# Laying the weights of a two-layer trunk out by block, partition and depth

## The chip, the cores and the metric

The kernel runs on the 8 cores of one Trainium2 chip, each core with its own sequence of the batch and its own 16 rows of the sample group; the cores exchange nothing. The metric is the device time of the slowest core, in microseconds (us).

## The reference

Two layers, then a final RMSNorm. Each layer, on 2048 rows of 1024 features a core (and on 16 sample rows beside them):

```python
h = rmsnorm(x, norm_g)
proj = einsum('btd,de->bte', h, w_in)          # w_in 1024 x 2560: a_in | a_gate | u | v | b_gate, 512 each
a_out = pool_mix(a_in) * silu(a_gate)          # trailing means over 2/4/8/16 rows, minus the row, then w_pool
vn = rmsnorm per head of v
b_out = u * (tril(w_s) @ vn + b_s) * silu(b_gate)   # chunks of 128 rows, 4 heads
y = x + concat(a_out, b_out) @ w_out           # w_out 1024 x 1024
```

## The kernel before

All weights come once from HBM as float32 and are cast to bfloat16 by the DMA on the way: `w_in` of a layer in five blocks of 512 columns (`load_win`, L307; order V, AIN, AGATE, BGATE, U), `w_out` in two halves (`load_wout`, L320). They stay in SBUF for the whole run. Every weight DMA is issued by GpSimd (`wdma`, L304), 16 of them in a row at the program's start, with two small `wpool` loads among them; `w_out` of layer 1 is loaded later, since its place serves as staging for small constants first. V of layer 0 comes in four pieces of two depth slices, AIN in two of four, every other block in one. A depth slice k is 128 rows of the 1024: partition p gets row 128 k + p.

The sequence's 16 tiles of 128 rows are worked in groups of four. `items` (L798) sets the order: group 0 layer 0 (item 0), group 1 layer 0 (item 1), group 0 layer 1, group 1 layer 1, and the same for groups 2 and 3. `run_item` (L841) does one: V projection, AIN with the pooling, AGATE, BGATE, U with the chunk mix, then the output projection `out_mm` (L960). The next group's norm runs inside: for item 0 (L976 to L992) the squares, the scale and the transposes `norm_tr` (L482) of tiles 4 to 7 stand between the pieces of the output projection, and each engine executes in this written order. So TensorE cannot begin item 1 before it has transposed tile 7 (L991).

SyncE issues the loads of x (`load_tile`, L289) and the small constants, in order: tiles 0 to 3 at once; `vg_bc0` behind the third V piece (L342), `wsk_h` behind the first AIN piece (L343), tiles 4 and 5 behind layer 0's U block, 6 and 7 behind the first half of its `w_out`:

```python
        for t in (4, 5):
            load_tile(t, deps=[wop[f"w0_{C_U}_0"]])
        for t in (6, 7):
            load_tile(t, deps=[wop["wout0_0"]])
```

Each of these loads must go through the same 16 DMA engines as the weights that are still queued by GpSimd (queue q0 in the profile; SyncE's is q1).

Of the kernel before, what the change touches and what calls it, by code (L numbers as in the profile page):

```python
# [6 lines left out]
F32 = mybir.dt.float32  # L7
BF16 = mybir.dt.bfloat16
# [8 lines left out]
D = 1024  # L17
# [3 lines left out]
DIN = 2560  # L21
# [127 lines left out]
def build_program():  # L149
# [12 lines left out]
    win_d = din("w_in", [2, D, DIN])  # L162
# [4 lines left out]
    wout_d = din("w_out", [2, D, D])  # L167
# [13 lines left out]
    with ExitStack() as es:  # L181
# [6 lines left out]
        win = [sb(f"win{l}", [128, 8, DIN], BF16) for l in range(2)]  # L188
        wout = [sb(f"wout{l}", [128, 8, D], BF16) for l in range(2)]
# [55 lines left out]
        stg = wout[1][:, :, :].rearrange("p k e -> p (k e)").bitcast(F32)  # L245
# [61 lines left out]
        def load_win(l, cb):  # L307
            src = win_d[l][:, cb:cb + 512].rearrange("(k p) e -> p k e", p=128)
            n = PIECES.get((l, cb), 1)
            for j in range(n):  # L310
                ks = slice(j * 8 // n, (j + 1) * 8 // n)
                wdma(win[l][:, ks, cb:cb + 512], src[:, ks, :], wbufs(l, cb, ks.start, ks.stop), f"w{l}_{cb}_{j}")
# [7 lines left out]
        def load_wout(l, deps=()):  # L320
            for hf in range(2):
                wdma(wout[l][:, :, hf * 512:(hf + 1) * 512],
                     wout_d[l][:, hf * 512:(hf + 1) * 512].rearrange("(k p) e -> p k e", p=128),
                     buf(f"wout{l}_{hf}"), f"wout{l}_{hf}", deps)
# [184 lines left out]
        def proj_fm(l, col0, bank=None, parts=HALVES):  # L509
            cb = (col0 // 512) * 512  # L510
            pf, pfb = bank or bankF.alloc()
            proj(l, cb, pf[:, 0:GT], pfb, lambda k: win[l][:, k, col0:col0 + 128], lambda k: hT[:, k, :],
                 [buf(f"hT{i}") for i in range(TPG)], parts)
            return pf, pfb

        def proj_tm(l, i, col0, bank=None, parts=HALVES):
            pf, pfb = bank or bankF.alloc()
            proj(l, col0, pf[:, :], pfb, lambda k: hT[:, k, i * 128:(i + 1) * 128],
                 lambda k: win[l][:, k, col0:col0 + 512], [buf(f"hT{i}")], parts)
            return pf, pfb  # L520

        def proj_s(l, col0):
            pf, pfb = bankF.alloc()
            proj(l, col0, pf[0:NS, :], pfb, lambda k: hTs[:, k, :], lambda k: win[l][:, k, col0:col0 + 512],
# [186 lines left out]
        def s_out(l):  # L711
            for hf in range(2):
# [3 lines left out]
                def f_o(h, pf=pf, s=s):  # L716
                    r = None
                    for k in range(8):
                        r = h.matmul(out=pf[0:NS, :], lhsT=mixTs[:, k, :], rhs=wout[l][:, k, s], start=(k == 0), stop=(k == 7))  # L719
# [121 lines left out]
        def run_item(n):  # L841
# [271 lines left out]
```

How the kernel before makes its waits and increments, by code:

```python
    def run_engine(self, e, h, sems):  # L124
        waited = {}
        for op in self.ops[e]:
            for d in op.deps:
                key, val = d.tok
                if waited.get(key, 0) < val:
                    h.wait_ge(sems[key], val)
                    waited[key] = val
            ins = op.fn(h)
            if op.dma is not None:
                ins.then_inc(sems[op.dma], 16)
            elif op.used:
                ins.then_inc(sems[e], 1)
# [911 lines left out]
def run_sync(S, h, sems):  # L1048
    waited = {}
    ops = S.ops[SP]
    for n, op in enumerate(ops):
        for d in op.deps:
            key, val = d.tok
            if waited.get(key, 0) < val:
                h.wait_ge(sems[key], val)
                waited[key] = val
        if n == len(ops) - 1:
            break
        ins = op.fn(h)
        if op.dma is not None:
            ins.then_inc(sems[op.dma], 16)
```

## Time and profile before

| what | value |
|---|---|
| median of 3 runs (lowest to highest) | 504.48 us (504.33 to 505.32) |
| the profiled execution's own time | 505.44 us |
| its span, slowest core (core 4) | 503.9 us |
| spans of the other cores | 498.2 to 503.8 us |
| TensorE (PE) busy | 467.4 us, 93% |
| VectorE (DVE) busy | 339.4 us, 67% |
| ScalarE (ACT) busy | 176.1 us, 35% |
| GpSimd (POOL) busy | 102.8 us, 20% |
| DMA moved | 36.85 MB in 22375 packets |

Busy shares are averages over the span. A DMA packet of a weight load is counted by what it writes (1024 bytes of bfloat16); it reads 2048 bytes. Times in timelines are from the span's start; in brackets stands how long the engine had been idle, and what ended that.

### The profile page before, as it was taken

Reading aid. Unit: us, or ns where it says so; the run is one execution under the profiler, and the core shown is the slowest. Engines: PE = TensorE matmul, PEld = TensorE weight load, DVE = VectorE, ACT = ScalarE, POOL = GpSimd, SP = SyncE. Lnnn points to the kernel's source line nnn. Section 1 sums busy time; section 2 is a strip of 40 time slices with the busy share of each in tenths; the row PEclk is TensorE's granted clock in tenths of the full one; section 3 lists DMA queues with packets and bytes.
Section 4 is the critical chain, followed back from the end, with each engine's and each line's share of the span. In section 5 each row is a group of like instructions: output and inputs, shape, how many; then the busy total and the mean of one; then the engine's idle time right before and its main releaser. Section 6 shows DMA issues by size and latency. Waiting matters only on the chain.

```text
span 503.9 us, 7706 instructions; the slowest of 8 cores (498.2 to 503.9 us)
## 1 busy us (share of the span) xinstructions
PE 467.4 (93%) x2382; PEld 214.3 (43%) x2428; DVE 339.4 (67%) x665; ACT 176.1 (35%) x294; POOL 102.8 (20%) x140
## 2 busy tenths in 40 slices
PE   2868998999999899999999999999999999999991
PEld 1423444444444345444444444444454444444440
DVE  3977528759766666876787757565764767886565
ACT  3224152480026402239133640023701380333044
POOL 8360012410051100251016100024000500161000
PEclk9999999999999899999999999999999999999996
DMA  7999999990059300550037000000000000220013
GB/s 191 150 166 152 210 189 200 167 120 2 0 86 147 60 1 1 169 169 1 2 95 240 3 5 1 0 1 27 4 1 0 1 1 1 85 105 2 1 42 125
DMA packets 22375, 36.85 MB, mean 73 GB/s; under 512 B 1664, under 2 KB 16384, under 8 KB 22304
## 3 DMA queue, kind: packets, MB, share of 16 engines
q0 software_dynamic: 14912, 14.94, 21.9%
q1 hardware_dynamic: 6704, 20.26, 13.7%
q10 hardware_dynamic: 720, 1.16, 0.7%
q8 instruction: 20, 0.33, 0.3%
q14 instruction: 19, 0.16, 0.1%
HBM read 42.06 MB, written 10.09 MB: 104 GB/s over the span
## 4 chain that ended last, share of the span: by engine, by line
PE 74%; DMA 7%; DVE 6%; issue 5%; ACT 3%; POOL 3%; ACTq 0%; DVEq 0%; POOLq 0%
PE pF L505 49%; PE pF L966 17%; DMA win<-w_in 7%; PE pT L489 2%; PE pF L950 2%; PE pF L947 2%; PE pF L719 1%; PE pF L918 1%; ACT vscr L757 1%; POOL win L305 1%; DVE Tt L546 1%; DVE xg L972 1%; DVE mix L938 1%; ACT vscr L464 1%; ACT hT L792 1%
## 5 line engine op out<-in xcount | busy, mean ns | idle before, releaser
L505 PE MATMUL pF<-hT,win 128*128 128x512 bf16 x1001 | 231.5, 382 | 7.6 <-DVE vn_sb L588 2.8
L505 PEld LDWEIGHTS pF<-hT,win 128*128 128x128 bf16 x1024 | 98.8, 98 | 123.5 <-issue 12.6
L966 PE MATMUL pF<-wout,mix 128*128 128x512 bf16 x497 | 112.8, 379 | 3.1 <-DVE wout L388 0.9
L966 PEld LDWEIGHTS pF<-wout,mix 128*128 128x128 bf16 x512 | 48.9, 98 | 58.5 <-issue 4.2
L578 POOL TENSOR_TENSOR ss<-ss,nhalf 128x4 f32<-128x4 f32 (+1 forms) x34 | 37.2, 1093 | 152.9 <-DVE ss L576 152.8
L505 PE MATMUL pF<-win,hT 128*128 128x512 bf16 x266 | 60.3, 379 | 1.6 <-DVE hT L493 1.3
L972 DVE TENSOR_TENSOR xg<-pF,xg 128x512 f32<-128x512 f32 x64 | 43.9, 688 | 21.2 <-PE pF L966 19.8
L464 ACT ACTIVATE vscr<-xg 128x1024 bf16<-128x1024 f32 x40 | 42.3, 1056 | 44.2 <-DVE xg L972 38.5
L479 ACT ACTIVATE hb<-xg,ssx 128x1024 bf16<-128x1024 f32 x28 | 32.0, 1144 | 66.8 <-PE pT L489 56.1
L473 POOL TENSOR_TENSOR ssx<-ssx,nhalf 128x1 f32<-128x1 f32 (+1 forms) x22 | 15.0, 682 | 187.1 <-DVE ssx L471 169.1
L569 ACT ACTIVATE vscr<-pF 128x512 f32<-128x512 f32 x32 | 19.1, 597 | 96.4 <-PE pF L505 65.5
L505 PEld LDWEIGHTS pF<-win,hT 128*128 128x128 bf16 x272 | 26.3, 98 | 33.1 <-issue 2.2
L555 DVE SCALAR_TENSOR_TENSOR d_sb<-Tt,a_sb 128x512 bf16<-128x512 f32 x32 | 22.1, 691 | 24.8 <-POOL halo L553 24.5
L897 ACT COPY a_sb<-pF 128x512 f32<-128x512 f32 x32 | 18.6, 585 | 57.7 <-DVE d_sb L555 17.6
L493 DVE TENSOR_TENSOR hT<-pT,cpk 128x1024 bf16<-128x1024 bf16 x32 | 38.2, 1215 | 0.5 <-PE pT L489 0.5
L921 DVE SCALAR_TENSOR_TENSOR mix<-pF,cpk,mix 128x512 bf16<-128x512 f32 x32 | 23.8, 748 | 20.4 <-PE pF L918 17.5
L938 DVE TENSOR_TENSOR mix<-pF,mix 128x512 bf16<-128x512 f32 x32 | 22.1, 692 | 22.0 <-PE pF L505 21.8
L588 DVE SCALAR_TENSOR_TENSOR vn_sb<-pF,ss,vg_bc 128x128 bf16<-128x128 f32 x120 | 33.8, 344 | 1.6 <-issue 0.4
L546 DVE TENSOR_TENSOR Tt<-Tt 128x512 f32<-128x512 f32 (+3 forms) x40 | 27.9, 697 | 4.5 <-DVE Tt L546 0.5
L572 DVE TENSOR_REDUCE ss<-vscr 128x4 f32<-128x512 f32 x32 | 21.8, 680 | 11.4 <-ACT vscr L569 11.4
L928 ACT ACTIVATE mix<-pF 128x512 bf16<-128x512 f32 x32 | 18.8, 593 | 23.4 <-PE pF L505 23.3
L955 DVE TENSOR_TENSOR mix<-pF,mix 128x512 bf16<-128x512 f32 x32 | 22.1, 689 | 2.5
(98 smaller groups left out, 340.4 us busy)
## 6 DMA issues: line engine op xcount, KB each, us to landing
xg<-x SPq DMA_DIRECT2D x16, 512.0 KB, 6.5
win<-w_in POOLq DMA_DIRECT2D x8, 1024.0 KB, 74.8
y<-xg SPq DMA_DIRECT2D x12, 512.0 KB, 3.2
wout<-w_out POOLq DMA_DIRECT2D x4, 1024.0 KB, 35.9
win<-w_in POOLq DMA_DIRECT2D x4, 256.0 KB, 14.1
win<-w_in POOLq DMA_DIRECT2D x2, 512.0 KB, 22.0
y<-hT SPq DMA_DIRECT2D x4, 256.0 KB, 2.5
y<-hT ACTq DMA_DIRECT2D x4, 256.0 KB, 2.7
```

The costliest lines, as they stand in the source:

```text
L464: S.emit(ACT, lambda h: h.activation(out=junk[:, 0:D], in_=xa, func=AF.Square, accum_out=ssx[:, c:c + 1]), reads=[xbuf(self.G, i), buf("ss ...
L479: S.emit(ACT, lambda h: h.activation(out=hb[:, i % NHB, :], in_=xa, func=AF.Copy, scale=rsx[:, c:c + 1]), reads=[xbuf(self.G, i), buf(f"rs ...
L493: S.emit(DVE, lambda h: h.tensor_tensor(out=hT[:, :, i * 128:(i + 1) * 128], in0=pt[:, :].rearrange("p (k t) -> p k t", k=8), in1=gT[:, l, ...
L505: r = h.matmul(out=out_ap, lhsT=lhsT(k), rhs=rhs(k), start=(k == 0), stop=(k == 7))
L546: S.emit(PENG, lambda h, dst=dst, src=src, c0=c_from, sh=shift: h.tensor_tensor(out=dst[:, c0:AW], in0=src[:, c0:AW], in1=src[:, c0 - sh:A ...
L555: S.emit(DVE, lambda h, src=src: h.scalar_tensor_tensor(out=d_sb[:, g, :], in0=src[:, HALO:AW], scalar=1.0 / w, in1=a_sb[:, sl, HALO:AW], ...
L578: S.emit(POOL, lambda h: h.tensor_tensor(out=rs4[0:nparts, c, :], in0=rs4[0:nparts, c, :], in1=nhalf[0:nparts, :], op=ALU.pow), reads=[rb, ...
L588: r = h.scalar_tensor_tensor(out=out[:, s], in0=pf[0:nparts, s], scalar=rs4[0:nparts, c, hh:hh + 1], in1=vg_bc[0:nparts, l, s], op0=ALU.mu ...
L921: S.emit(DVE, lambda h: h.scalar_tensor_tensor(out=mix[:, g, :], in0=pf[:, 0:GT], scalar=psc[:, l, g, :], in1=mix[:, g, :], op0=ALU.mult, ...
L938: S.emit(DVE, lambda h, pf=pf, hh=hh: h.tensor_tensor(out=mix[:, 4 + hh, :], in0=pf[:, 0:GT], in1=mix[:, 4 + hh, :], op=ALU.mult), reads=[ ...
L966: r = h.matmul(out=pf[:, :], lhsT=mix[:, k, i * 128:(i + 1) * 128], rhs=wout[l][:, k, hf * 512:(hf + 1) * 512], start=(k == 0), stop=(k == 7))
L972: S.emit(DVE, lambda h: h.tensor_tensor(out=xa[:, hf * 512:(hf + 1) * 512], in0=pf[:, :], in1=xa[:, hf * 512:(hf + 1) * 512], op=ALU.add), ...
```

## The change

In HBM the host stores `w_in` as [layer, block, partition, depth x column], and `w_out` in the same way with two blocks. In SBUF the tiles get the block as their first free dimension: [128, 5, 8, 512] in place of [128, 8, 2560], and [128, 2, 8, 512] in place of [128, 8, 1024]. So the part of a block that one partition gets (8 depth slices x 512 columns) is one run, on both sides: 16 KB of float32 in HBM and 8 KB of bfloat16 in SBUF, where it was eight runs of 2 KB and 1 KB. A V piece becomes a run of 4 KB, an AIN piece one of 8 KB (float32). The number of DMAs, their bytes, their order, what waits for them, and every matmul's shape are the same.

```diff
--- before.py
+++ after.py
@@ -159,12 +159,12 @@
     x_d = din("x", [SEQ, D])
     xs_d = din("xs", [NS, D])
     st_d = din("st", [2, NS, PB, WA])
-    win_d = din("w_in", [2, D, DIN])
+    win_d = din("win_h", [2, 5, 128, 4096])
     wpool_d = din("wpool_h", [2, 128, 512])
     psc_d = din("pool_scale", [2, WA])
     vng_d = din("v_norm_g", [2, WB])
     bs_d = din("b_s", [2, 4, 128])
-    wout_d = din("w_out", [2, D, D])
+    wout_d = din("wout_h", [2, 2, 128, 4096])
     fng_d = din("fng", [1, D])
     cpk_d = din("cpk_h", [128, NCPK])
     wsk_d = din("wsk_h", [128, 1152])
@@ -185,8 +185,8 @@
         def ps(name, shape, dt):
             return es.enter_context(nc.psum_tensor(name, list(shape), dt))
 
-        win = [sb(f"win{l}", [128, 8, DIN], BF16) for l in range(2)]
-        wout = [sb(f"wout{l}", [128, 8, D], BF16) for l in range(2)]
+        win = [sb(f"win{l}", [128, 5, 8, 512], BF16) for l in range(2)]
+        wout = [sb(f"wout{l}", [128, 2, 8, 512], BF16) for l in range(2)]
         wpool = sb("wpool", [128, 2, 4, 128], BF16)
         wsT = sb("wsT", [128, 2, 4, 128], BF16)
         xg = sb("xg", [128, NSLOT, D], F32)
@@ -242,7 +242,7 @@
         ds_s = smpb[Q[3], 0:512]
         mixTs = hTs
 
-        stg = wout[1][:, :, :].rearrange("p k e -> p (k e)").bitcast(F32)
+        stg = wout[1][:, :, :, :].rearrange("p a k e -> p (a k e)").bitcast(F32)
         mask = stg[:, 0:128]
         wsf = [stg[:, 128 + 512 * l:640 + 512 * l].rearrange("p (h i) -> p h i", h=4) for l in range(2)]
         st_sb = [stg[:, 1152 + 960 * l:2112 + 960 * l].rearrange("p (r j) -> p r j", r=PB) for l in range(2)]
@@ -305,11 +305,11 @@
             wop[key] = S.emit(POOL, lambda h, o=out_ap, i=in_ap: h.dma_start(out=o, in_=i), writes=[wb], dma=key, deps=deps)
 
         def load_win(l, cb):
-            src = win_d[l][:, cb:cb + 512].rearrange("(k p) e -> p k e", p=128)
+            src = win_d[l, cb // 512].rearrange("p (k e) -> p k e", k=8)
             n = PIECES.get((l, cb), 1)
             for j in range(n):
                 ks = slice(j * 8 // n, (j + 1) * 8 // n)
-                wdma(win[l][:, ks, cb:cb + 512], src[:, ks, :], wbufs(l, cb, ks.start, ks.stop), f"w{l}_{cb}_{j}")
+                wdma(win[l][:, cb // 512, ks, :], src[:, ks, :], wbufs(l, cb, ks.start, ks.stop), f"w{l}_{cb}_{j}")
 
         def wbufs(l, cb, k0=0, k1=8):
             return [buf(f"win{l}_{cb}_{q}") for q in range(k0 // 2, k1 // 2)]
@@ -319,8 +319,7 @@
 
         def load_wout(l, deps=()):
             for hf in range(2):
-                wdma(wout[l][:, :, hf * 512:(hf + 1) * 512],
-                     wout_d[l][:, hf * 512:(hf + 1) * 512].rearrange("(k p) e -> p k e", p=128),
+                wdma(wout[l][:, hf, :, :], wout_d[l, hf].rearrange("p (k e) -> p k e", k=8),
                      buf(f"wout{l}_{hf}"), f"wout{l}_{hf}", deps)
 
         def stage(*a, **k):
@@ -509,19 +508,19 @@
         def proj_fm(l, col0, bank=None, parts=HALVES):
             cb = (col0 // 512) * 512
             pf, pfb = bank or bankF.alloc()
-            proj(l, cb, pf[:, 0:GT], pfb, lambda k: win[l][:, k, col0:col0 + 128], lambda k: hT[:, k, :],
+            proj(l, cb, pf[:, 0:GT], pfb, lambda k: win[l][:, cb // 512, k, col0 - cb:col0 - cb + 128], lambda k: hT[:, k, :],
                  [buf(f"hT{i}") for i in range(TPG)], parts)
             return pf, pfb
 
         def proj_tm(l, i, col0, bank=None, parts=HALVES):
             pf, pfb = bank or bankF.alloc()
             proj(l, col0, pf[:, :], pfb, lambda k: hT[:, k, i * 128:(i + 1) * 128],
-                 lambda k: win[l][:, k, col0:col0 + 512], [buf(f"hT{i}")], parts)
+                 lambda k: win[l][:, col0 // 512, k, :], [buf(f"hT{i}")], parts)
             return pf, pfb
 
         def proj_s(l, col0):
             pf, pfb = bankF.alloc()
-            proj(l, col0, pf[0:NS, :], pfb, lambda k: hTs[:, k, :], lambda k: win[l][:, k, col0:col0 + 512],
+            proj(l, col0, pf[0:NS, :], pfb, lambda k: hTs[:, k, :], lambda k: win[l][:, col0 // 512, k, :],
                  [buf("hTs")])
             return pf, pfb
 
@@ -716,7 +715,7 @@
                 def f_o(h, pf=pf, s=s):
                     r = None
                     for k in range(8):
-                        r = h.matmul(out=pf[0:NS, :], lhsT=mixTs[:, k, :], rhs=wout[l][:, k, s], start=(k == 0), stop=(k == 7))
+                        r = h.matmul(out=pf[0:NS, :], lhsT=mixTs[:, k, :], rhs=wout[l][:, s.start // 512, k, :], start=(k == 0), stop=(k == 7))
                     return r
                 S.emit(PE, f_o, reads=[buf("mixTs"), buf(f"wout{l}_{hf}")], writes=[pfb])
                 S.emit(DVE, lambda h, pf=pf, s=s: h.tensor_tensor(out=xs_sb[:, s], in0=pf[0:NS, :], in1=xs_sb[:, s], op=ALU.add),
@@ -964,7 +963,7 @@
                         r = None
                         for k in range(4 * hk, 4 * hk + 4):
                             r = h.matmul(out=pf[:, :], lhsT=mix[:, k, i * 128:(i + 1) * 128],
-                                         rhs=wout[l][:, k, hf * 512:(hf + 1) * 512], start=(k == 0), stop=(k == 7))
+                                         rhs=wout[l][:, hf, k, :], start=(k == 0), stop=(k == 7))
                         return r
                     S.emit(PE, f, reads=[buf(f"mix{k}") for k in range(4 * hk, 4 * hk + 4)] + [buf(f"wout{l}_{hf}")],
                            writes=[pfb])
@@ -1081,6 +1080,10 @@
                   w_s=f(w_s), b_s=f(b_s), w_out=f(w_out), fng=f(final_norm_g).reshape(1, D))
     ident, inv, m01, mask = _consts()
     shared["wpool_h"] = np.ascontiguousarray(shared.pop("w_pool").transpose(0, 2, 1, 3).reshape(2, 128, 512))
+    shared["win_h"] = np.ascontiguousarray(shared.pop("w_in").reshape(2, 8, 128, 5, 512).transpose(0, 3, 2, 1, 4)
+                                           .reshape(2, 5, 128, 4096))
+    shared["wout_h"] = np.ascontiguousarray(shared.pop("w_out").reshape(2, 8, 128, 2, 512).transpose(0, 3, 2, 1, 4)
+                                            .reshape(2, 2, 128, 4096))
     shared["cpk_h"] = np.ascontiguousarray(np.concatenate(
         [ident, shared.pop("norm_g").reshape(2, 8, 128).transpose(2, 0, 1).reshape(128, 16),
          shared["pool_scale"].reshape(2, 4, 128).transpose(2, 0, 1).reshape(128, 8), inv, m01], axis=1))
```

No instruction moves on any engine; the shapes of the weight DMAs change. GpSimd's queue at the program's start before (partitions x runs x elements; L305 is the helper that issues):

```order
L305 DMA win<-w_in 128x2x512 x4
L305 DMA win<-w_in 128x4x512 x2
L305 DMA win<-w_in 128x8x512
L305 DMA wpool<-wpool_h 128x512
L305 DMA win<-w_in 128x8x512 x2
L305 DMA wout<-w_out 128x8x512 x2
```

and now:

```order
L305 DMA win<-win_h 128x1024 x4
L305 DMA win<-win_h 128x2048 x2
L305 DMA win<-win_h 128x4096
L305 DMA wpool<-wpool_h 128x512
L305 DMA win<-win_h 128x4096 x2
L305 DMA wout<-wout_h 128x4096 x2
```

Nothing moved in the queue; the program states each partition's part as one run of 1024, 2048 or 4096 elements where it stated 2, 4 or 8 runs of 512.

## Rows read from the trace of the kernel before

**Rows 1.** The page: span, and busy time of TensorE

```profile
span 503.9 us, 7706 instructions; the slowest of 8 cores (498.2 to 503.9 us)
PE 467.4 (93%) x2382; PEld 214.3 (43%) x2428; DVE 339.4 (67%) x665; ACT 176.1 (35%) x294; POOL 102.8 (20%) x140
```

**Rows 2.** Busy time by stretch: PE, PEld, DVE, ACT, POOL, PEclk, DMA share, GB/s

```profile
40.00:60.00 20.00, 18.41 (x90) 7.96 (x90) 12.32 (x25) 6.78 (x11) 0.00 (x0) 1.00 1.11 186
60.00:80.00 20.00, 17.49 (x101) 8.29 (x102) 9.97 (x18) 7.93 (x12) 2.22 (x4) 1.00 1.09 205
100.00:504.00 404.00, 386.51 (x1979) 177.26 (x2015) 276.17 (x533) 142.56 (x240) 68.41 (x91) 0.98 0.19 47
```

**Rows 3.** Timeline of TensorE in item 0: start, duration, instructions [idle before]

```profile
19.23 5.77 PE L505 MATMUL pF<-win,hT 128*128 128x512 bf16 x26 [0.76 <-DVE hT L493]
...
36.66 7.07 PE L505 MATMUL pF<-hT,win 128*128 128x512 bf16 x32 [1.64 <-ACT a_sb L897]
45.21 3.61 PE L505 MATMUL pF<-hT,win 128*128 128x512 bf16 x15 [1.48 <-DMA win<-w_in]
...
70.85 3.61 PE L966 MATMUL pF<-wout,mix 128*128 128x512 bf16 x16 [0.85 <-DMA wout<-w_out]
...
80.51 0.61 PE L489 MATMUL pT<-ident,hb 128*128 128x128 bf16 x8
```

**Rows 4.** The page: DMA packets of the whole span, and weight queue q0

```profile
DMA packets 22375, 36.85 MB, mean 73 GB/s; under 512 B 1664, under 2 KB 16384, under 8 KB 22304
q0 software_dynamic: 14912, 14.94, 21.9%
```

**Rows 5.** DMA, 51.3 to 55.0 us: between two x issues and their first packet

```profile
q0 software_dynamic: 611, 0.62, 115.7%
issues: line engine op xcount, KB each, median us to landing
xg<-x SPq DMA_DIRECT2D x2, 512.0 KB, 8.6
```

**Rows 6.** DMA, 56 to 60 us, and (last line) 65 to 70 us: x beside weights

```profile
DMA packets 465, 1.10 MB, mean 275 GB/s; under 512 B 31, under 2 KB 252, under 8 KB 465
q1 hardware_dynamic: 230, 0.87, 60.7%
q0 software_dynamic: 235, 0.23, 42.3%
...
DMA packets 486, 1.15 MB, mean 230 GB/s; under 512 B 29, under 2 KB 264, under 8 KB 486
```

**Rows 7.** DMA of core 0, 144.1 to 144.9 us: 16 runs of 28 KB

```profile
DMA packets 31, 0.46 MB, mean 574 GB/s; under 512 B 15, under 2 KB 15, under 8 KB 15
q1 hardware_dynamic: 31, 0.46, 140.6%
```

**Rows 8.** Timeline of SyncE's queue, tiles 4 to 7 of x

```profile
51.30 9.89 SPq L292 DMA_DIRECT2D xg<-x  x4
```

**Rows 9.** DMA issues of 60.0 to 62.5 us: tiles 6 and 7

```profile
xg<-x SPq DMA_DIRECT2D x2, 512.0 KB, 9.5
```

**Rows 10.** Timeline of ScalarE: squares and scales of tiles 4 to 7

```profile
59.08 1.06 ACT L464 ACTIVATE vscr<-xg 128x1024 bf16<-128x1024 f32 x1 [5.68 <-DMA xg<-x]
...
74.36 1.04 ACT L464 ACTIVATE vscr<-xg 128x1024 bf16<-128x1024 f32 x1
...
76.59 1.15 ACT L479 ACTIVATE hb<-xg,ssx 128x1024 bf16<-128x1024 f32 x1 [1.10 <-POOL ssx L473]
```

**Rows 11.** DMA, 7.6 to 13.4 us: tiles 2 and 3 beside the first weights

```profile
q1 hardware_dynamic: 290, 1.03, 54.8%
q0 software_dynamic: 326, 0.32, 48.5%
```

**Rows 12.** DMA issue of vg_bc, and the vector operation that needs it

```profile
vg_bc<-v_norm_g SPq DMA_DIRECT2D x1, 256.0 KB, 9.0
...
27.28 1.13 DVE L588 SCALAR_TENSOR_TENSOR vn_sb<-pF,ss,vg_bc 128x128 bf16<-128x128 f32 x4
```

**Rows 13.** SyncE's first issues, and the DMA view from 1 to 3 us

```profile
1.06 2.41 SPq L292 DMA_DIRECT2D xg<-x  x4
...
GB/s 0 0 0 0 0 0 0 0 0 0 0 0 0 0 0 0 0 0 0 0 0 0 0 0 82 82 82 82 0 0 328 0 164 164 0 82 0 82 82 328
```

## The prediction

> **What bounds the kernel now.** I read the page first, then the busy times by stretch, the timelines of TensorE, ScalarE and SyncE in item 0, and the DMA view of short stretches. TensorE is busy for 467.4 of 503.9 us [rows 1], and from 100 us on for 386.5 of 404 [rows 2]: behind item 1's start it has nearly no slack, so a shift of item 1 goes to the end one for one. Before 100 us the DMA engines are full (share 1.09 to 1.11) and TensorE waits here and there, 2.5 of the 20 us from 60 to 80 [rows 2]. The change touches only how the weights come in, so what matters is item 0, up to the transposes of tile 7, which start at 80.51 and open item 1 [rows 3].
>
> In item 0, TensorE waits for a weight block itself twice: 1.48 us for BGATE at 45.21 and 0.85 us for the second half of w_out at 70.85 [rows 3]. Everything else that it waits for (x tiles through the norm, pooling, banks) is not a weight. So **all that faster weights can give is 2.3 us**.
>
> **What a packet costs.** The weight queue moves 14912 packets in the run [rows 4]: 14336 of the blocks and halves, 256 of wpool, 320 for the semaphores of 20 DMAs. wpool's four groups of 128 elements are stated as one run and make one packet per partition. I take it that the new runs, too, become one packet each, of up to 16 KB read. Alone, q0 did 611 packets in 3.7 us on 16 engines [rows 5]: 3.7 x 16 / 611 = 0.097 us per packet, so eight of them 0.775 us. That is the upper bound for a 16 KB packet (nothing gained). The lower bound comes from the long runs that the trace has: 16 of 28 KB had a share of 140.6% of 16 engines in 0.8 us [rows 7], 1.125 us each with the semaphores, so 16 KB take 0.643 us. They have no cast, but they are long; I lean to them two to one, as the rows nearest in length: **0.687 us**. Per 2 KB that is 0.086 instead of 0.097, a saving of 0.011 us (0 to 0.017).
>
> The Trainium skill ("DMA: Bandwidth & Descriptors", Why small descriptors are slow) gives a fixed overhead of some 3 cycles per packet over beats of 32 bytes, which for 2 KB is 3 in 67, 4.5%; by that a 16 KB packet takes 0.745 us. The 28 KB runs show 17%. By the page x tile 7 below would come 2.6 us later than by my value.
>
> **Part 1: weights earlier.** Up to U, an engine takes 328 packets of 2 KB (5 blocks of 64 and 8 of wpool). 328 x 0.011 = 3.6 us earlier at U (0 to 5.6). BGATE then is there before TensorE asks, and so is w_out. This alone gives up to 2.3 us.
>
> **Part 2: x tiles 2 and 3 later.** From 7.6 to 13.4 us the queues alternate, 290 packets of x's queue against 326 [rows 11]; less the semaphores about 16 x packets per engine are left beside V's first pieces. A V run now reads 4 KB, 0.16 to 0.19 us instead of 0.097, so tile 3 comes 16 x 0.064 to 0.097 = 1.0 to 1.5 us later, and with it the V projection's full pace at 19.23 [rows 3]. AGATE's last matmul, at 36.66 + 7.07 = 43.7, moves to 45.0. BGATE started at 45.21 because it had to wait, so the shift costs nothing and takes most of that 1.48 us away: BGATE starts at 45.0, 0.2 earlier, and with the 0.85 us at 70.85 TensorE is 1.05 us ahead there.
>
> vg_bc, behind the third V piece, lands 9.0 us after its issue of 17.8, at 26.8, and is needed at 27.28 [rows 12]. Its 8 packets per engine now stand beside AIN runs of 8 KB, 8 x 0.25 = 2 us more, against a need 1.3 us later: 0.2 us late, at most 1. I cost it at nothing because part 3 leaves TensorE more slack than that; without part 3 it would be 0 to 1 us. GpSimd issues the same DMAs and waits for nothing of them; the later constants (rest of wsk, state, vg_bc1) are needed only from item 1's end on.
>
> **Part 3: x tiles 4 to 7 crowded out.** This decides. From 56 to 60 us x packets (4 KB) and weight packets went strictly one to one, 230 to 235 [rows 6]. Without the semaphores a pair took 4 x 16 / 217 = 0.295 us, from 65 to 70 us 5 x 16 / 228 = 0.350. Less the weight packet, x's own is 0.20 to 0.25. If the alternation is one packet for one, and nothing in the rows shows otherwise, each x packet now stands behind a 16 KB weight packet: a pair takes 0.687 + 0.225 = 0.912 us (0.643 + 0.20 = 0.84 to 0.775 + 0.25 = 1.03). Tiles 4 to 7 are 4 x 8 = 32 packets per engine: 29.2 us (27.0 to 32.8).
>
> Their start: the first two are issued at 51.3, when U has landed [rows 8], and no x packet is seen for 3.7 us [rows 5]. With U 3.6 us earlier: 47.7 + 3.7 = 51.4. w_out's first half lands some 7 us after U, while tile 4 is on its way, so tiles 6 and 7 follow without a gap. Tile 7 lands at 51.4 + 29.2 = **80.6 us** (45.7 + 3.7 + 27.0 = 76.4 to 51.3 + 3.7 + 32.8 = 87.8). Before, it landed at about 61 + 9.5 = 70.5 [rows 8, 9].
>
> The need: its square began at 74.36 and its scale ended at 76.59 + 1.15 = 77.74 [rows 10], 3.4 us, and the transposes came at 80.51 only by their place. So it may land at 77.1. At 80.6 it is 3.5 us late. Tiles 4, 5 and 6 come 7.3 us apart before it, at 58.7, 66.0 and 73.3; only tile 6's square, at 70.8 before, is pushed, and it is done before tile 7 arrives. The gain of 1.05 us only makes TensorE wait longer there.
>
> **Sum:** -0 (parts 1 and 2 end inside that wait) + 3.5 us. Against the profiled execution (505.44 us, core 4) that is 508.9, against the median of the runs, 0.96 lower, 504.48 + 3.5 = **508.0 us**. Its own range is tile 7 on time (503.4) to 87.8 - 77.1 = 10.7 us late (515.2).
>
> **Rivals.**
>
> *Weights early and x in time.* The engine arbitrates by bytes, or long runs are cut into packets of 8 KB read or less. With 8 KB (0.34 + 0.225) x 32 = 18 us, and tile 7 lands near 70, in time. Then the 1.05 us stand: 503.4 us, and at best 2.3 us, 502.2, if tile 3 isn't delayed. For it: no row shows a cast of more than 1 KB. Against it: the 28 KB runs are one packet each [rows 7], and the one to one of rows 6 and 11 holds although x's packets read twice the bytes.
>
> The Trainium skill ("DMA: Bandwidth & Descriptors", Queues, rings and completion order) has an engine drain a packet of some 9 to 17 descriptors before it turns to another ring. By that rule x would already stand behind 18 KB or more of weights per turn, and one 16 KB run in their place would cost it nothing: 503.4 us as well. The trace disagrees, with 230 to 235 and two tiles landed in 8.6 us. I give it 0.02 of this rival's 0.24.
>
> *Nothing to see.* The runs are cut to what they are now, or tile 7's lateness and the gain are both under 1 us: 504.5.
>
> *A longer entry.* The 3.7 us between issue and first packet may be a number of packets queued ahead, not a time. The first x of the program, issued at 1.06, was seen in the 25th of 40 slices between 1 and 3 us, at 2.2 [rows 13], 1.2 us later, so 2.5 us are 26 weight packets; 26 of 0.687 are 17.9. Tile 7 then lands at 96, 18.9 late: 523.4 us. It decides as soon as more than a few 16 KB packets stand ahead. For it: the same 3.7 us each time under load. Against it: 2.5 us are as well a fixed number of bytes.
>
> **Chances.** x crowded out as forecast, over 1 us late: 0.50. Weights early and x in time: 0.24. Nothing to see: 0.19. Longer entry: 0.07. A measurement of this kernel tells about 0.2%, 1.0 us, from no change (its three runs spread over 1.0). So faster 0.24, same 0.19, slower 0.57. The range from 503.0 to 516.0 holds the forecast's case with its bounds, the middle case and most of the faster one; it leaves out the long entry and the best end of the faster case.
>
> **What would show it.** The q0 packets fall from 14912 to 2880 (18 DMAs of blocks, pieces and halves x 128 runs, 256 of wpool, 320 semaphores). Tile 4's and 5's loads take 11 us and more from issue to landing instead of 8.6. ScalarE's square of tile 7 starts at its landing, near 80.6, with an idle "DMA xg<-x" before it, and TensorE's transposes behind it near 84. The waits for BGATE and w_out are gone. It is wrong if q0 still has about 15000 packets, if x beside weights is no slower than 0.35 us a pair, or if TensorE reaches item 1 before 81 us.

## The result and the profile after

The changed kernel takes 516.88 us (median of 4 executions, 516.24 to 517.17). The kernel before, run beside it on the same chip, takes 504.9 us (median of 4, 504.33 to 506.42). The ratio is **1.0237, interval 1.0216 to 1.0257**: slower by 2.4%, 12.0 us. The forecast was 508.0, range 503.0 to 516.0. Direction and place were right; the loss is over three times the 3.5 us of the sum, and the time lies 0.9 us outside the range. In some executions a few cores have a lower granted clock and take some per cent longer; all times, ratios and means below leave such executions and cores out.

Table of the two profiled executions, each on its slowest core:

| | before (core 4) | after (core 0) |
|---|---|---|
| profiled execution / span, us | 505.44 / 503.9 | 517.17 / 515.6 |
| TensorE busy | 467.4 (93%) | 471.3 (91%) |
| packets in the weight queue q0 | 14912 | 2880 |
| tile 7's square starts | 74.36 | 87.25 |
| item 1's first matmul | 80.95 | 96.06 |
| from there to the end | 422.9 | 419.5 |

The page of after, against [rows 1] and [rows 4]: span, busy time, the TensorE clock in 40 slices, the DMA queues and the heads of the chain that ended last.

```profile
span 515.6 us, 7752 instructions; the slowest of 8 cores (512.7 to 515.6 us)
PE 471.3 (91%) x2428; PEld 215.4 (42%) x2428; DVE 339.0 (66%) x665; ACT 176.1 (34%) x294; POOL 97.0 (19%) x140
PEclk9899996799999999999999999999999999999997
DMA packets 10343, 36.85 MB, mean 71 GB/s; under 512 B 1664, under 2 KB 2048, under 8 KB 8736
q0 software_dynamic: 2880, 14.94, 17.6%
q1 hardware_dynamic: 6704, 20.26, 12.3%
PE 70%; DMA 15%; DVE 6%; issue 3%; ACT 3%; POOL 2%; ACTq 0%; DVEq 0%; SPq 0%; POOLq 0%
```

q0 has exactly the 2880 packets that were forecast for one packet per run, so the change does what it says. The clock is under 0.8 only in the seventh and eighth slice, some 77 to 103 us, and in the last one, where the program ends. The share of DMA in the chain is 15%.

Busy time by stretch in item 0 (PE, PEld, DVE, ACT, POOL, PEclk, DMA share, GB/s), against [rows 2]:

```profile
40.00:60.00 20.00, 20.00 (x101) 8.92 (x99) 13.97 (x29) 6.32 (x10) 1.30 (x3) 1.00 1.00 176
60.00:80.00 20.00, 15.75 (x87) 7.15 (x84) 4.61 (x9) 5.74 (x8) 1.11 (x2) 1.00 1.02 206
80.00:100.00 20.00, 8.76 (x43) 4.47 (x44) 8.91 (x13) 4.16 (x6) 1.19 (x3) 0.66 0.99 197
```

From 40 to 60 us TensorE is now without a gap on this core. The rows of before are those of core 4, busy for 18.41 of these 20 us; core 4 is busy for 19.89 of them now, without its wait for BGATE. In before seven of the eight cores wait for a weight somewhere in item 0, in after none does. From 60 to 100 it is idle for 4.25 + 11.24 = 15.5 us, and the clock from 80 to 100 is 0.66. The DMA engines are as full as ever. Timeline of TensorE over the same place, against [rows 3]:

```profile
21.34 7.11 PE L504 MATMUL pF<-win,hT 128*128 128x512 bf16 x26 [0.54 <-DVE hT L492]
...
33.80 14.84 PE L504 MATMUL pF<-hT,win 128*128 128x512 bf16 x68 [0.98 <-DVE vn_sb L587]
...
75.25 1.89 PE L965 MATMUL pF<-wout,mix 128*128 128x512 bf16 x8
91.24 1.01 PE L488 MATMUL pT<-ident,hb 128*128 128x128 bf16 x8 [14.09 <-DVE hT L492]
92.04 3.62 PE L965 MATMUL pF<-wout,mix 128*128 128x512 bf16 x8
95.46 0.76 PE L488 MATMUL pT<-ident,hb 128*128 128x128 bf16 x8
96.06 7.07 PE L504 MATMUL pF<-win,hT 128*128 128x512 bf16 x32
```

There are three things to see. V's long run of matmuls begins at 21.34; on core 4 of before it was 19.23, on core 4 of after it is 20.38. One wait of 14.09 us stands at 91.24, ahead of tile **6**'s transposes. And the 8 matmuls behind it take 3.62 us, where 8 of the same shape take 1.89 at 75.25. Next the squares on ScalarE (L463) and the vector engine behind them (L470 is the statistics of a tile, L971 an addition of an output, L492 the multiply that empties a transpose bank), against [rows 10]:

```profile
63.49 1.06 ACT L463 ACTIVATE vscr<-xg 128x1024 bf16<-128x1024 f32 x1 [10.27 <-DMA xg<-x]
71.31 1.06 ACT L463 ACTIVATE vscr<-xg 128x1024 bf16<-128x1024 f32 x1 [3.88 <-DMA xg<-x]
78.70 1.06 ACT L463 ACTIVATE vscr<-xg 128x1024 bf16<-128x1024 f32 x1 [4.04 <-DMA xg<-x]
87.25 1.06 ACT L463 ACTIVATE vscr<-xg 128x1024 bf16<-128x1024 f32 x1 [4.84 <-DMA xg<-x]
...
88.50 0.15 DVE L470 TENSOR_SCALAR ssx<-ssx 128x1 f32<-128x1 f32 x1 [7.39 <-ACT vscr L463]
88.67 1.29 DVE L971 TENSOR_TENSOR xg<-pF,xg 128x512 f32<-128x512 f32 x2
89.88 2.34 DVE L492 TENSOR_TENSOR hT<-pT,cpk 128x1024 bf16<-128x1024 bf16 x2
```

All four squares now wait for "DMA xg<-x", 7.4 to 8.6 us apart. So x is crowded out, tile after tile. The last three rows show why TensorE stood still: VectorE waits 7.39 us at tile 7's statistics, and behind it in its queue stand the two multiplies that free the two transpose banks.

The DMA view of after from 64 to 72 us, packets, MB, share of 16 engines, against [rows 6]:

```profile
DMA packets 299, 1.63 MB, mean 203 GB/s; under 512 B 33, under 2 KB 33, under 8 KB 168
q0 software_dynamic: 148, 1.07, 78.3%
q1 hardware_dynamic: 151, 0.55, 24.0%
```

Still one to one, 148 to 151, with packets of 16 KB against 4 KB. Less some 16 semaphores in each queue a pair takes 8 x 16 / 132 = 0.97 us, where it took 0.295 to 0.350.

Equal counts would also come of turns of several packets each. The single packets of the trace decide that. On core 0, from 56 to 84 us, there are 475 packets of x. In the 10 ns at their ends 486 weight packets start, where other stretches of 10 ns near by hold some 80, by chance. Of starts of another x packet there are 92, no more than chance. So on one engine one packet of x is followed by one of weights.

### The profile page after: what moved, and what is told of

The parts are those of the page before. It is cut to its first block, busy times and chain, and to the rows that moved or that the text cites. A ratio compares the mean times of both kernels' runs of the same rounds, so it can differ in the third digit from the quotient of the medians.

```text
span 515.6 us, 7752 instructions; the slowest of 8 cores (512.7 to 515.6 us)
## 1 busy us (share of the span) xinstructions
PE 471.3 (91%) x2428; PEld 215.4 (42%) x2428; DVE 339.0 (66%) x665; ACT 176.1 (34%) x294; POOL 97.0 (19%) x140
## 2 busy tenths in 40 slices
DMA packets 10343, 36.85 MB, mean 71 GB/s; under 512 B 1664, under 2 KB 2048, under 8 KB 8736
## 3 DMA queue, kind: packets, MB, share of 16 engines
q0 software_dynamic: 2880, 14.94, 17.6%
## 4 chain that ended last, share of the span: by engine, by line
PE 70%; DMA 15%; DVE 6%; issue 3%; ACT 3%; POOL 2%; ACTq 0%; DVEq 0%; SPq 0%; POOLq 0%
PE pF L504 45%; PE pF L965 17%; DMA wout<-wout_h 10%; DMA xg<-x 6%; PE pT L488 2%; PE pF L949 1%; PE pF L946 1%; PE pF L718 1%; ACT vscr L756 1%; PE pF L917 1%; DVE Tt L545 1%; POOL win L305 1%; DVE xg L971 1%; ACT hT L791 1%; DVE mix L937 1%
## 5 line engine op out<-in xcount | busy, mean ns | idle before, releaser
L965 PE MATMUL pF<-wout,mix 128*128 128x512 bf16 x512 | 116.3, 383 | 1.5 <-DVE wout L387 0.9
L463 ACT ACTIVATE vscr<-xg 128x1024 bf16<-128x1024 f32 x40 | 42.3, 1058 | 61.6 <-DVE xg L971 38.5
L504 PE MATMUL pF<-win,hT 128*128 128x512 bf16 x272 | 62.2, 385 | 1.2 <-DVE hT L492 1.1
L971 DVE TENSOR_TENSOR xg<-pF,xg 128x512 f32<-128x512 f32 x64 | 43.9, 688 | 23.1 <-PE pF L965 21.7
L492 DVE TENSOR_TENSOR hT<-pT,cpk 128x1024 bf16<-128x1024 bf16 x32 | 38.2, 1215 | 0.5 <-PE pT L488 0.5
L937 DVE TENSOR_TENSOR mix<-pF,mix 128x512 bf16<-128x512 f32 x32 | 22.1, 692 | 22.0 <-PE pF L504 21.9
L488 PE MATMUL pT<-ident,hb 128*128 128x128 bf16 x256 | 20.0, 229 | 17.8 <-DVE hT L492 14.1
L571 DVE TENSOR_REDUCE ss<-vscr 128x4 f32<-128x512 f32 x32 | 21.7, 680 | 12.7 <-ACT vscr L568 12.7
L488 PEld LDWEIGHTS pT<-ident,hb 128*128 128x128 bf16 x256 | 17.0, 103 | 24.0 <-issue 21.9
```

The source lines that it names most:

```text
L463: S.emit(ACT, lambda h: h.activation(out=junk[:, 0:D], in_=xa, func=AF.Square, accum_out=ssx[:, c:c + 1]), reads=[xbuf(self.G, i), buf("ss ...
L488: r = h.transpose(out=pt[:, k * 128:(k + 1) * 128], in_=hb[:, j, k * 128:(k + 1) * 128], identity=ident[:, :])
L492: S.emit(DVE, lambda h: h.tensor_tensor(out=hT[:, :, i * 128:(i + 1) * 128], in0=pt[:, :].rearrange("p (k t) -> p k t", k=8), in1=gT[:, l, ...
L504: r = h.matmul(out=out_ap, lhsT=lhsT(k), rhs=rhs(k), start=(k == 0), stop=(k == 7))
L937: S.emit(DVE, lambda h, pf=pf, hh=hh: h.tensor_tensor(out=mix[:, 4 + hh, :], in0=pf[:, 0:GT], in1=mix[:, 4 + hh, :], op=ALU.mult), reads=[ ...
L971: S.emit(DVE, lambda h: h.tensor_tensor(out=xa[:, hf * 512:(hf + 1) * 512], in0=pf[:, :], in1=xa[:, hf * 512:(hf + 1) * 512], op=ALU.add), ...
```

## The experiments

Of the eight cores each is a little different, so the readings below are means over all eight, taken from the timelines of each core's profile. "V" is the start of V's long run of matmuls, "sq 4 to 7" the starts of ScalarE's squares of x tiles 4 to 7, "item 1" that of item 1's first matmul, "rest" the time from there to the core's end. The last columns are the median time and the ratio, with its interval, to the kernel before, which ran on the same chip in the same job (504.5 to 505.5 us by its medians).

```
                                V    sq4  sq5  sq6  sq7  item 1 rest   us      ratio
before                          18.8 57.9 66.3 69.6 73.2 79.9   421.7  504.9   1
after                           21.0 62.0 70.3 77.8 85.6 94.4   419.5  516.88  1.0237 1.0216..1.0257
e1 short beside x               20.9 56.6 67.6 70.9 74.5 81.7   421.1  506.97  1.0036 1.0018..1.0053
e2 x in the weight queue        21.1 54.0 68.2 71.4 75.0 82.3   419.4  504.81  1.0010 0.9986..1.0035
e3 after, statistics later      21.1 61.3 69.7 77.1 84.8 89.1   420.5  514.66  1.0179 1.0152..1.0206
e4 after, matmuls in the wait   20.9 61.7 69.9 77.5 85.4 92.5   419.6  514.73  1.0194 1.0163..1.0224
e5 long beside x alone          18.7 64.1 72.1 80.0 88.0 96.5   419.5  518.19  1.0268 1.0236..1.0299
e6 before, statistics later     18.9                72.7 77.8   421.6  503.40  0.9979 0.9959..0.9999
e8 e2 + e3                      20.6 53.4 67.7 70.9 74.5 78.7   420.1  501.26  0.9933 0.9908..0.9959
e9 e2, V's pieces short         18.8                73.8 80.4   419.5  504.34  0.9994 0.9969..1.0019
e10 e8, all x in that queue     18.1                75.0 79.3   420.1  501.97  0.9933 0.9907..0.9959
e11 e9 + e3                     18.9                74.0 78.3   420.6  501.14  0.9925 0.9902..0.9948
e12 before, as e8               19.1                73.4 78.3   421.4  502.63  0.9958 0.9943..0.9974
e13 runs of 8 KB                21.1 58.4 67.2 70.5 74.2 81.4   419.5  504.33  0.9992 0.9972..1.0012
```

**e1: the weights that go beside tiles 4 to 7 (w_out, layer 1) as before; layer 0's w_in in long runs.**

```diff
+            if l not in (0,):
+                src = wino_d[l][:, cb:cb + 512].rearrange("(k p) e -> p k e", p=128)
...
-                wdma(wout[l][:, hf, :, :], wout_d[l, hf].rearrange("p (k e) -> p k e", k=8),
+                wdma(wout[l][:, hf, :, :], wouto_d[l][:, hf * 512:(hf + 1) * 512].rearrange("(k p) e -> p k e", p=128),
```

> The changed kernel, SBUF layout and layer 0's w_in as in the change, but w_out and layer 1's w_in read from the old layout in HBM, so that the packets beside x tiles 4 to 7 read 2 KB again. Theory (one x packet per weight packet, of whatever length): tiles 4 to 7 land as before, tile 7 near 70, item 1 starts at 79 to 81 us, total 503.5 to 505.5. Rival (something else in the new layout, such as SBUF's, or tiles 2 and 3 being late): 512 or more. The rest of the span would be 420 to 423 us, as before.

Measured: 506.97 us, ratio 1.0036. Item 1 comes at 81.7 instead of 94.4, so of the 14.5 us by which the change delays item 1, 12.7 are **the crowding of tiles 4 to 7**. It didn't come back to the kernel before, as an interval above 1 says, and the time lies over the 503.5 to 505.5 that were expected. Item 1 is 1.8 later than there, and V starts 2.1 later: the early part, which I had costed at nothing, costs.

**e5: the counterpart, long runs only in w_out and layer 1, so beside tiles 4 to 7.**

```diff
+            if l not in (1,):
+                src = wino_d[l][:, cb:cb + 512].rearrange("(k p) e -> p k e", p=128)
```

> The complement of the run with short packets beside tiles 4 to 7: layer 0's w_in is read from the old layout (2 KB packets), w_out and layer 1's w_in in the long runs. Theory (nearly all of the loss is x tiles 4 to 7): the V projection starts near 19 as before, tile 7 lands near 86, item 1 starts at 92 to 94, total 514 to 516. Rival (the early part matters more than the 1.7 us that the other half showed): below 512.

Measured: 518.19 us, over the 514 to 516 that were expected, and slower than the whole change. V starts at 18.7 as before, tile 7's square at 88.0. The part beside x therefore costs all that the change costs. The early part's 2 us don't add to it, because TensorE waits at item 1 in any case. That e5 is the slower one fits its x issues: SyncE issues tile 4 on all cores' mean at 50.6 here and at 49.1 in after, 1.4 us later, and the 512 packets of tiles 4 to 7 take 32.2 us instead of 31.2. Tile 7's square is 2.4 later. The crowding in its DMA view, 64 to 72 us:

```profile
q0 software_dynamic: 147, 1.08, 79.9%
q1 hardware_dynamic: 145, 0.54, 22.2%
```

**e13: the dose. Blocks in two DMAs of 4 depth slices, so that a packet reads 8 KB.** Tiles 4 and 5 start behind U's second piece.

```diff
-        PIECES = {(0, C_V): 4, (0, C_AIN): 2}
+        PIECES = {(l, cb): 4 if (l, cb) == (0, C_V) else 2 for l in range(2) for cb in WIN_ORDER}
...
+                    wdma(wout[l][:, hf, 0:4, :], wsrc[:, 0:4, :], buf(f"wo0{hf}a"), f"wout0_{hf}a", deps)
+                    wdma(wout[l][:, hf, 4:8, :], wsrc[:, 4:8, :], buf(f"wo0{hf}b"), f"wout0_{hf}", deps)
```

> The changed layout, but each block and half of w_out is loaded by two DMAs of four depth slices, so that a packet reads 8 KB instead of 16. Theory (x waits one weight packet per packet): a pair takes 0.37 + 0.22 = 0.59 us instead of 0.96, a tile 4.7 instead of 7.7; tile 7 lands near 71 to 75, item 1 starts at 81 to 84, total 504.5 to 508. Rival (x's share is set by bytes or by a fixed number of packets in flight, and the length is not what matters): tile 7 still after 84, total over 513.

Measured: ratio 0.9992, tile 7's square at 74.2, item 1 at 81.4. The DMA view from 62 to 66 us:

```profile
q0 software_dynamic: 129, 0.48, 66.9%
q1 hardware_dynamic: 135, 0.49, 34.5%
```

Less some 14 semaphores a pair takes 4 x 16 / 115 = 0.56 us. With 2 KB it was 0.295 to 0.350, with 16 KB 0.97: **the alternation is by packets, at each of the three lengths tried**, and 32 packets of 0.56 end in time where 32 of 0.97 don't. (The forecast's faster rival had 0.565 for this pair. Its own reason, that the 16 KB runs would be cut into such packets, was wrong.)

**e2: tiles 4 to 7 in GpSimd's queue,** 4 and 5 ahead of w_out and 6 and 7 between its halves, so that x competes with no other queue.

```diff
-        load_wout(0)
+        for t in (4, 5):
+            load_tile(t, eng=POOL)
+        load_wout(0, mid=(6, 7))
...
-        for t in (4, 5):
-            load_tile(t, deps=[wop[f"w0_{C_U}_0"]])
-        for t in (6, 7):
-            load_tile(t, deps=[wop["wout0_0"]])
```

> The changed kernel, but x tiles 4 and 5 are issued by GpSimd between U and w_out, 6 and 7 between w_out's halves, in the weights' own queue and with no wait. Theory (only the alternation of two queues crowds x out): a tile costs its own 8 packets of 0.17 us, 1.4 us each; tile 5 lands by 54, tile 7 by 63; no waits for x, item 1 starts at 79 to 80, total 503 to 504.5. Rival (long packets hold the engines whoever asks): tile 7 after 80, total over 512.

Measured: ratio 1.0010, no difference that can be told. Tile 4 is there at 54.0 and tile 7 never waited for, yet item 1 starts at 82.3, 2.4 later than before and not at the 79 to 80 that were expected. On core 7 of e2 VectorE waits early for vg_bc, and TensorE late for a transpose bank:

```profile
31.54 1.13 DVE L588 SCALAR_TENSOR_TENSOR vn_sb<-pF,ss,vg_bc 128x128 bf16<-128x128 f32 x4 [1.04 <-DMA vg_bc<-v_norm_g]
...
81.98 0.61 PE L489 MATMUL pT<-ident,hb 128*128 128x128 bf16 x8 [2.28 <-DVE hT L493]
```

The first is looked at in e9, the second in e3 and e8 below.

**e9: e2 with V's four pieces of layer 0 in short runs again.**

```diff
+            if (l, cb) == (0, C_V):
+                src = wino_d[l][:, cb:cb + 512].rearrange("(k p) e -> p k e", p=128)
```

> As the run with x tiles 4 to 7 in the weights' queue, but layer 0's V pieces are read from the old layout (packets of 2 KB read beside x tiles 0 to 3). Theory (V's 4 KB packets crowd x tiles 2 and 3 in the same way): the V projection's full pace starts near 19 instead of 21, item 1 near 80.3 instead of 82.3, total 502.9 to 503.8. Rival (the later start is absorbed behind it, as I had reckoned): 505.3.

Measured: V at 18.8 as before, item 1 at 80.4 against e2's 82.3. (The means are of six of its cores.) V's long pieces beside tiles 2 and 3 thus cost 1.9 us on item 1; what of that is x's packets and what vg_bc's, no run separates. The time, 504.34 us, misses the 502.9 to 503.8 that were expected, and the ratio, 0.9994, overlaps e2's: on the whole time the 1.9 us are not shown.

**e3: the statistics of tile 3 of the next item behind its first transposes.** In item 0's tail, VectorE's operation on tile 7's row sums (L470) moves behind the multiply of tile 4. Everything is computed as in the changed kernel.

```diff
-                    nrm.rstd(i, 1)
                     if i < 3:
+                        nrm.rstd(i, 1)
                         nrm.scale(i)
...
                 norm_tr(*nx, 0)
+                nrm.rstd(3, 1)
```

> The changed kernel with tile 7's small statistics operation on VectorE moved behind the gT multiply of tile 4's transposes. Theory (that operation, which needs tile 7's square, stands ahead of the multiplies that free the transposes' banks, and so makes tile 6's transposes wait for tile 7): tile 7 still lands near 87, but tile 6's transposes go at 83, and item 1 starts near 91.5 to 92.5 instead of 94.4 in the mean of cores; total 512.5 to 514.5. Rival (the chain runs over ScalarE's scale of tile 7 alone, as I had reckoned): no change, 516.9.

Measured: 514.66 us, item 1 at 89.1 instead of 94.4, though tile 7's square is only 0.8 earlier, at 84.8. TensorE in e3, core 2:

```profile
83.94 1.01 PE L488 MATMUL pT<-ident,hb 128*128 128x128 bf16 x8 [6.47 <-DVE hT L492]
84.75 3.43 PE L965 MATMUL pF<-wout,mix 128*128 128x512 bf16 x8
90.17 0.61 PE L488 MATMUL pT<-ident,hb 128*128 128x128 bf16 x8 [1.99 <-ACT hb L478]
```

Tile 6's transposes no longer wait for tile 7, and the last wait is for ScalarE's scale of tile 7, the path that I had measured the need by. From the square to item 1 it is now 4.3 us on the mean of the cores, against 8.8. So **tile 7 was needed through VectorE's queue**. Item 1 gains more (5.3 us) than the median time does (2.2). The rest is 1.0 us longer, which leaves 4.3; the profiled execution took 513.27, 3.9 less than after's, but is the lowest of its four.

**e6: the same edit on the kernel before.**

```diff
-                    nrm.rstd(i, 1)
                     if i < 3:
+                        nrm.rstd(i, 1)
...
+                nrm.rstd(3, 1)
```

> The kernel before, with only tile 7's small statistics operation moved behind tile 4's gT multiply. If that operation holds tile 6's transposes back already in the kernel before (TensorE idles 0.5 to 1.7 us there, by core), the idle goes: item 1 starts 0.5 to 1.5 us earlier, total 503.5 to 504.8. Rival (the order matters only when tile 7 is late): 505.1, no change.

Measured: ratio 0.9979 [0.9959, 0.9999], item 1 at 77.8 against 79.9. Item 1 gains 2 us, of which 0.5 is tile 7's square being earlier (72.7 against 73.2). The whole time gains 0.2%, at the edge of what can be told.

**e4: 60 unused matmuls in the wait.** They stand behind the third tile's second half of the output, ahead of tile 6's transposes, and write a free bank.

```diff
+                    for _ in range(60):
+                        r = h.matmul(out=pF[ib][:, :], lhsT=mix[:, 0, 0:128], rhs=mix[:, 0, :], start=True, stop=True)
```

> The changed kernel with 60 matmuls without use (13 us) where TensorE waits for tile 7, ahead of tile 6's transposes, into a bank that is free. Theory (TensorE's granted clock falls to 0.5 in that wait and stays there for some us of work): clock 1.0 throughout item 0's end, item 1 starts 1.7 to 2.5 us earlier, and the total is 514.5 to 515.2 unless a lower clock later takes it back. Rival (the low clock costs nothing, as the work there waits anyway): 516.9.

Measured: 514.73 us, 2.2 under after. Tile 7 is as late as there (85.4), but item 1 comes 1.9 us earlier. Busy time by stretch, core 1:

```profile
60.00:80.00 20.00, 19.70 (x109) 9.14 (x107) 6.00 (x11) 5.25 (x7) 1.11 (x2) 1.00 1.02 206
80.00:100.00 20.00, 20.00 (x106) 9.59 (x105) 10.59 (x19) 5.73 (x9) 2.82 (x4) 1.00 1.02 198
```

The clock from 80 to 100 is 1.00 on all eight cores instead of 0.66. Of the loss, **some 2 us are the slow clock behind the long wait**, not the wait.

**e8: e2 and e3's edit together, on the changed kernel.**

```diff
+            load_tile(t, eng=POOL)
+        load_wout(0, mid=(6, 7))
...
+                nrm.rstd(3, 1)
```

> Long packets, x tiles 4 to 7 in the weights' queue, and the statistics operation of tile 7 moved. There TensorE still idled 2.28 us ahead of tile 6's transposes on every core looked at; that goes, item 1 starts near 80.0 (mean of cores, after 82.3), total 502.8 to 503.6. Rival (what remains is tiles 2 and 3 alone): 505.

Measured: **501.26 us, ratio 0.9933 [0.9908, 0.9959]**, faster than both kernels and than the 502.8 to 503.6 that were expected. TensorE, core 1, has no wait from the output matmuls to item 1:

```profile
77.66 0.61 PE L489 MATMUL pT<-ident,hb 128*128 128x128 bf16 x8
78.11 1.89 PE L966 MATMUL pF<-wout,mix 128*128 128x512 bf16 x8
79.83 0.61 PE L489 MATMUL pT<-ident,hb 128*128 128x128 bf16 x8
```

**e12: the same two edits on the kernel before, with its short runs.**

```diff
+            load_tile(t, eng=POOL)
+        load_wout(0, mid=(6, 7))
...
+                nrm.rstd(3, 1)
```

> The kernel before (short packets everywhere) with the two other edits: x tiles 4 to 7 in the weights' queue, the statistics operation moved. It says what long packets are worth by themselves. If they bring the weights in earlier and the rest of the span runs on a higher clock (rest 419.4 us with long packets and x in queue, 420 to 423 with short ones): 503.5 to 504.8, slower than the same edits with long packets and short V pieces. Rival (long packets are worth nothing): 502.5 or less.

Measured: 0.9958 [0.9943, 0.9974]. Here too item 1 comes at 78.3. What the new layout is worth once x is out of its way is e8 against e12, 501.26 against 502.63 us. The two intervals overlap, but both hold the same runs of the kernel before. Compared directly, three of e8's four executions (500.41, 501.25, 501.26, 501.97) lie under all ten of e12 (501.64 to 504.19). That points to a gain of some 1.4 us, though from four executions; it lies behind item 1, which starts 0.4 us later in e8.

**e11: e8 with V's pieces short.**

```diff
+            if (l, cb) == (0, C_V):
+                src = wino_d[l][:, cb:cb + 512].rearrange("(k p) e -> p k e", p=128)
...
+                nrm.rstd(3, 1)
```

> All edits that helped together: long runs, V's pieces short, x tiles 4 to 7 in the weights' queue, tile 7's statistics moved. Theory (the gains add): V at full pace near 19, item 1 near 77.5 on undisturbed cores, the rest 419.4 to 421, total 499.3 to 500.8, under the 501.3 of the same with long V pieces. Rival (with tile 3 early another chain bounds, so nothing adds): 501.3.

Measured: 0.9925 [0.9902, 0.9948]; item 1 at 78.3 against e8's 78.7. The gains did not add to the 499.3 to 500.8 us that were expected: the rival holds.

**e10: e8 with tiles 0 to 3 in the weight queue as well.**

```diff
-            load_tile(t)
+            load_tile(t, eng=POOL)
```

> Long runs, every x tile in the weights' queue, tiles 0 to 3 ahead of the first weight, statistics moved. Theory (in one queue tiles 0 to 3 have the engines for themselves): tile 3 lands at 10 to 11.5 instead of 13 to 15, the V projection's full pace comes at 17.5 to 18.5, item 1 at 76 to 77, total 498.5 to 500. Rival (GpSimd's issue starts later and slower than SyncE's, and V's first piece comes later): V not before 19, total 501 or more.

Measured: 0.9933. V starts at 18.1, the earliest of all, but item 1 at 79.3 instead of the expected 76 to 77, and nothing is gained over e8. Why the head start is gone by item 1 was not looked into further.

## Why the prediction was wrong in size

It was right that the change slows the kernel, through tiles 4 to 7 and nothing else, and that x and weights alternate packet by packet. Its sum, by its own steps:

| step | forecast | measured |
|---|---|---|
| U lands, so tile 4 is issued | 3.6 us earlier | 49.7 to 49.1 on the cores' mean, 0.6 earlier |
| issue to first x packet | 3.7 us | 4.0 on the cores' mean, in before as in after |
| 32 pairs of packets | 29.2 us (27.0 to 32.8) | 31.4, from the first x packet to the end of the last |
| last x packet to tile 7's square | not a step | 85.6 - 49.1 - 4.0 - 31.4 = 1.1 |
| need of tile 7 | lands by 77.1, 2.74 after its square | by its square, no slack |
| clock behind the wait | not a step | about 2 |
| rest of the span | unchanged | 421.7 to 419.5, 2.2 less |

On the cores' means the forecast is 49.7 - 3.6 + 3.7 + 29.2 = 79.0 for tile 7, against a need of 73.2 + 2.74 = 75.9: 3.1 us. Add 3.0 for U, 0.3 for the entry, 2.2 for the pairs, 1.1 behind the last packet, 2.7 for the slack and 2.0 for the clock, less 2.2 for the rest: 12.2, where 12.0 was measured. So three steps failed: the price of a 16 KB packet (U and the pairs, 5.2 us of the miss), the need of tile 7 (2.7), and the clock behind the wait, which I had put at nothing without a reason (2.0).

**What a packet costs: mis-sized, and it failed twice.** I took 0.687 us for a weight packet of 16 KB, leaning to the 28 KB runs two to one. While tiles 4 to 7 came, such packets took 0.74 to 0.76 us, by the mean of each core, and a pair took 31.4 / 32 = 0.98 us. q0's own share from 64 to 72 us says the same: 0.783 x 8 x 16 / 132 = 0.76. That is next to my upper bound, 0.775: on the mean a run of 16 KB costs about as much as eight of 2 KB do in [rows 5]. The same price is in part 1. With next to nothing saved per byte U can't be early, and tile 4 was issued 0.6 us earlier instead of 3.6. (These are two executions. Over more of them tile 4 is issued at 49.2 to 50.6 with short runs, in before, e5 and e6, and at 48.5 to 49.1 with long ones, in after, e1, e3 and e4: 1.1 us earlier on the mean.)

Why the 28 KB runs misled can be seen in part. Half of the 16 KB packets on core 0 took 0.63 us or less, as I had priced them, though they cast, so the cast is not the cause; the others took up to 2.0 us. [rows 7] showed 16 packets of 1.125 us at a quick moment. The other 16 of the same load took up to 2.15 us, and over the cores of before the mean of one was 1.2 to 2.9 us, which is 0.70 us and more for 16 KB. Bytes read per us agree as well: 329 GB/s in [rows 5] (2 KB runs alone), 331 in [rows 6], 339 in after from 64 to 72 us. What holds them there no run tries.

The Trainium skill ("DMA: Bandwidth & Descriptors", Why small descriptors are slow) was the better guide. By its 3 cycles per packet a 16 KB packet would take 0.745 us, an estimate, against 0.74 to 0.76 measured. Two readings of the prediction are off here. The 3.6 us of part 1 took the full saving for all 328 packets, but the pieces of V and AIN become runs of 4 and 8 KB only: 248 packets fewer x 0.088 / 7 is 3.1 us. And by that rule of the Trainium skill tile 7 would come 4.1 us later than by my value (32 x 0.058, and 3.6 - 1.4 at U), not 2.6.

**Part 1** otherwise did as said. The waits for weights are gone from the timelines of all cores. They are worth nothing, since the wait at tile 7 swallows them.

**Part 2, "it costs nothing".** In the sum that holds: e5, without it, is not faster. By itself it doesn't: e1 and e2 have it without the crowding, and item 1 is 1.8 and 2.4 us later in them than before. I forecast tile 3 1.0 to 1.5 us late and V started 2.2 late.

**Part 3, the need.** The step "so it may land at 77.1" failed. I followed tile 7 through ScalarE to its own transposes and not through VectorE's queue, where its statistics stand ahead of tile 4's and 5's multiplies. Row by row it was in the trace of before. Its VectorE and TensorE, core 4:

```profile
75.60 0.15 DVE L471 TENSOR_SCALAR ssx<-ssx 128x1 f32<-128x1 f32 x1 [2.44 <-ACT vscr L464]
75.77 1.29 DVE L972 TENSOR_TENSOR xg<-pF,xg 128x512 f32<-128x512 f32 x2
76.98 2.34 DVE L493 TENSOR_TENSOR hT<-pT,cpk 128x1024 bf16<-128x1024 bf16 x2
...
78.34 0.61 PE L489 MATMUL pT<-ident,hb 128*128 128x128 bf16 x8 [1.26 <-DVE hT L493]
```

TensorE already waited 1.26 us on this path. e3 and e6 show it by taking it away.

**The rest.** It was taken as unchanged and is 2.2 us shorter in after. It is as short (419.4 to 419.6) in e2, e4, e5, e9 and e13, which have w_out and layer 1 in long runs, and 421.1 to 421.7 in before, e1, e6 and e12, which don't; the four with the statistics later and long runs (e3, e8, e10, e11) stand between, at 420.1 to 420.6. One place of it can be seen. In before, then in after, where TensorE waits in item 2:

```profile
170.87 0.38 PE L918 MATMUL pF<-d_sb,wpool 128*128 128x512 bf16 x1 [2.40 <-DVE vnf L588]
171.09 3.29 PE L505 MATMUL pF<-hT,win 128*128 128x512 bf16 x8
```

```profile
184.39 0.38 PE L917 MATMUL pF<-d_sb,wpool 128*128 128x512 bf16 x1 [1.68 <-DVE vnf L587]
184.60 1.89 PE L504 MATMUL pF<-hT,win 128*128 128x512 bf16 x8
```

The wait is 0.7 us shorter, and no slow clock follows it (1.89 us for 8 matmuls, not 3.29). So it is on every core: 2.4 us in before, e1, e6 and e12, 1.7 in all runs with long runs there. After this wait the clock falls on five of the eight cores of before, and on four, seven and five of e1, e6 and e12; with long runs it falls on none. On the cores' means after is 1.1 us shorter up to the end of this wait, and 1.2 behind it. That long runs shorten the rest is a pattern over the runs; why the wait is shorter was not tried.

**The rivals.** "Weights early and x in time" is refuted by 148 to 151 packets of 16 KB and 4 KB. So is the rule of the Trainium skill ("DMA: Bandwidth & Descriptors", Queues, rings and completion order) of some 9 to 17 descriptors per turn, if a packet of the trace is a descriptor: the engines changed queue behind each one. "A longer entry" fell as well. From the issue to the first x packet it is 4.0 us on the cores' mean in both kernels (3.7 to 4.7 in before, 3.7 to 4.3 in after), though the packets ahead read eight times as much. It did not go by the number of packets. "Nothing to see" had a cut into short packets or a small lateness; neither is there.

## What to carry to other kernels

Before making one queue's runs longer, look for what shares its DMA engines at that time: the engines gave each queue one packet per turn, so a packet of the other queue waited for 16 KB instead of 2, and this kernel bore 8 KB per run but not 16. Either keep runs short there, or put the urgent loads into the same queue at their place (with the statistics moved, 0.7% under the kernel before). And to find when a tile is needed, follow every engine that touches it, with what stands behind it in that engine's queue, not only the chain of its own data.

## What the runs showed of the hardware that was not expected

- Two queues on one set of DMA engines took turns, one packet each, at every length tried: 230 to 235 (x's 4 KB beside 2 KB reads), 135 to 129 (beside 8 KB), 151 to 148 (beside 16 KB). A pair took 0.295 to 0.350, 0.56 and 0.97 us.
- A weight packet that reads 16 KB took 0.74 to 0.76 us on the mean beside x, half of core 0's 0.63 or less; eight of 2 KB took 0.775 alone. A packet of 28 KB took 1.06 us at the least, and 1.2 to 2.9 on the mean of a core.
- The first packet of an x load came 4.0 us after its issue on the cores' mean, beside 2 KB runs as beside 16 KB runs.
- In a wait of 14 us TensorE's granted clock fell to 0.5 (its 1.2 GHz level). On core 0 it stood there from 82.1 to 95.8 us, so for 4.6 us into the work, which took some 2 us more for it; with matmuls in the wait it stayed at 1.00 and those 2 us came back (e4).
